# Two decoder layers and two mixers on one core: the first attention as 64 steps in four phases, with the projections cut into pieces inside the steps

## The reference

```python
h = rmsnorm(x, ln1_g[i]) @ w_in[i]
(fq, fk, fv, ff, dq, dk, dv, c_q, c_kv, k_r) = jnp.split(h, split_points, axis=-1)
o_fox = fox_group(fq, fk, fv, ff, fgate_b[i])             # 4 heads of 64, causal, forget bias
o_diff = diff_group(dq, dk, dv, ...)                      # 4 heads, 2 softmaxes each, values of 128
o_mla = mla_group(c_q, c_kv, k_r, ...)                    # 4 heads, 64 + 32 rotary rows, values of 64
x = x + jnp.concatenate([o_fox, o_diff, o_mla], axis=-1) @ w_o[i]
# one block of 128 queries, in every group:
sc = jnp.einsum('bhqd,bhkd->bhqk', qb, k).astype(jnp.float32) * scale
p = jax.nn.softmax(sc + bias_fn(qi, ki), axis=-1).astype(v.dtype)
return jnp.einsum('bhqk,bhkd->bhqd', p, v)
# diff_group, at its end:
o = o1 - lam.astype(o1.dtype) * o2
o = rmsnorm(o, norm_g) * (1.0 - lam_init)
```

## Time and profile before

| | us |
|---|---|
| median of 3 runs (2925.74 to 2937.4) | 2934.0 |
| profiled execution, its own time | 2937.45 |
| its span | 2935.7 |
| PE busy | 2672.3 (91%) |
| DVE, ACT, POOL busy | 1091.8, 985.0, 1032.7 |
| chain that ended last, share of PE | 85% |
| first attention, layer 0, from the first split weight of `cq` to the norm `ln2` | 31.0 to 393.5 |
| the same stages, layer 1 | 775.5 to about 1137 |

### The profile page before, as it was taken

How to read it: one execution, slowest core, us unless ns; L and a number is a source line. 1 busy time by engine, 2 the same in 40 slices (tenths; PEclk the granted TensorE clock), 3 DMA queues, 4 the chain that set the end, 5 groups by cost and what they waited for, 6 DMA issues and landing times.

```text
span 2935.7 us, 34302 instructions
## 1 busy us (share of the span) xinstructions
PE 2672.3 (91%) x13358; PEld 2173.4 (74%) x13358; DVE 1091.8 (37%) x2040; ACT 985.0 (34%) x1811; POOL 1032.7 (35%) x567
## 2 busy tenths in 40 slices
PE   6989889999998988999968999999999899898888
PEld 4866678888776667888846877887878787786666
DVE  2035359730202544984015022241011243255564
ACT  3324344432332434444223132221223222244442
POOL 4341245664434114566442222222322132321121
PEclk9977899999998789999988999999999999999999
DMA  4210135322321013532321100111110021120000
GB/s 157 82 34 1 51 131 193 122 97 90 106 88 41 1 37 120 189 136 90 101 67 44 51 15 22 51 58 58 58 36 29 8 65 57 45 75 29 29 30 29
DMA packets 54513, 199.69 MB, mean 68 GB/s; under 512 B 6288, under 2 KB 6288, under 8 KB 53584
## 3 DMA queue, kind: packets, MB, share of 16 engines
q1 hardware_dynamic: 51696, 188.13, 19.1%
q10 hardware_dynamic: 2656, 9.37, 0.9%
HBM read 194.72 MB, written 2.10 MB: 67 GB/s over the span
## 4 chain that ended last, share of the span: by engine, by line
PE 85%; DVE 5%; ACT 4%; POOL 4%; issue 2%; DMA 0%; ACTq 0%; DVEq 0%; POOLq 0%
PE ps L490 59%; PE ps L520 12%; PE ps L736 5%; PE ps L820 4%; PE ps L619 2%; POOL wl L2033 1%; PE ps L950 1%; ACT wh L987 1%; DVE norm_sq L1520 1%; POOL norm_acc L2046 1%; POOL norm_sq L2149 0%; PE ps L641 0%; PE ps L743 0%; PE ps L935 0%; PE ps L934 0%
## 5 line engine op out<-in xcount | busy, mean ns | idle before, releaser
L2033 POOL TENSOR_TENSOR wl<-wring,wh 128x1024 fp32r<-128x1024 f32 (+2 forms) x305 | 756.8, 2481 | 1302.4 <-ACT wh L987 1291.9
L987 ACT ACTIVATE wh<-wring 128x1024 fp32r<-128x1024 f32 (+2 forms) x305 | 316.6, 1042 | 898.1 <-PE ps L490 889.7
L490 PE MATMUL ps<-hh,wh 128*128 128x512 f32 x1480 | 587.3, 397 | 32.7 <-POOL wl L2033 16.7
L490 PE MATMUL ps<-hl,wh 128*128 128x512 f32 x1480 | 584.9, 395 | 0.0
L490 PE MATMUL ps<-hh,wl 128*128 128x512 f32 x1480 | 584.3, 395 | 0.0
L490 PEld LDWEIGHTS ps<-hh,wh 128*128 128x128 f32 x1480 | 282.3, 191 | 99.0 <-issue 19.2
L490 PEld LDWEIGHTS ps<-hh,wl 128*128 128x128 f32 x1480 | 282.2, 191 | 61.0
L490 PEld LDWEIGHTS ps<-hl,wh 128*128 128x128 f32 x1480 | 282.7, 191 | 58.9 <-issue 0.5
L520 PE MATMUL ps<-arena 128*128 128x512 f32 (+8 forms) x496 | 237.2, 598 | 3.1 <-DVE aq_s L1901 1.5
L1556 DVE CUSTOM_DVE_ANT_0 arena<-arena 128x1024 f32<-128x1024 f32 x96 | 188.7, 1966 | 8.6 <-DVE arena L1690 0.3
L490 PE MATMUL ps<-wh,hh 128*128 128x256 f32 x544 | 156.7, 288 | 12.5 <-POOL wl L2033 4.7
(11 more groups left out here) (266 smaller groups left out, 4538.8 us busy)
## 6 DMA issues: line engine op xcount, KB each, us to landing
wring<-wts SPq DMA_DIRECT2D x284, 512.0 KB, 3.5
arena<-wts SPq DMA_DIRECT2D x48, 512.0 KB, 4.4
wring<-wts SPq DMA_DIRECT2D x18, 384.0 KB, 2.9
xL<-xt SPq DMA_DIRECT2D x1, 2048.0 KB, 9.7
arena<-tab SPq DMA_DIRECT2D x1, 2048.0 KB, 16.7
arena<-cv ACTq DMA_DIRECT2D x2, 1024.0 KB, 4.9
arena<-tab ACTq DMA_DIRECT2D x1, 2048.0 KB, 7.9
out_t<-xL ACTq DMA_DIRECT2D x8, 256.0 KB, 2.0
```

The source lines that it names most:

```text
L490: mm = nc.tensor.matmul(o[0], a, b, start=start and k == first and j == 0, stop=stop and k == last and j == 2)
L987: nc.scalar.activation(wh[:, sn % SPLIT_SLOTS, :kn * w], raw(u)[:, :kn * w], ACT.Copy).then_inc(act_done, tick("act", ("hi", u)))
L2033: G.tensor_tensor(wl[:, sn % SPLIT_SLOTS, :kn * w], raw(u)[:, :kn * w], wh[:, sn % SPLIT_SLOTS, :kn * w].bitcast(F32), ALU.subtract).then_inc(
```

## The change

- **Order of the units.** `unit1` gives four phases of 16 steps: fox, diff heads 0 and 1, diff heads 2 and 3, mla. Inside a phase the query block i is the outer loop, so every phase has its own four steps for each i.
- **Projections in the steps.** Ahead of the steps only cq, ckv, two `qk` jobs, the first `v` job, and the four forget rows remain. A new function `fill1(s)` puts a piece at the end of each PE step: in phases 0 and 1 a quarter of the next phase's `qk` job pair (12 products of 512 columns) or an eighth of its `v` job (12 of 256 columns); in phase 2 `uq`, `ukv`, the turned fox and diff outputs and the first of the output projection; in phase 3 more of it. `wo` is cut by input rows into three parts (features 0 to 511, 512 to 767, 768 to 1023), each added to `xL` by its own DVE add.
- **Differential pairs.** The second softmax of a pair is scaled by -lam times the ratio of the row sums and added to the first, in SBUF (`mix`, three DVE instructions). Only the sum is transposed and multiplied with the values: 48 units of T and PV instead of 64.
- **Fox mask.** The mask comes from PE as one more product (identity by mask, 128 columns) into the scores' bank; POOL's sixteen bias additions are gone.
- **Rotary rows.** The swapped columns are computed by the projection itself (32 more output rows), so the ten transfers and most of POOL's additions are gone; DVE does three 32 x 512 instructions for each mla head instead.
- **Buffers.** The step buffers lie in `arena`, no longer over `wh` and `wl`, so weights are split during the steps. T and PV run one step later (s-3, s-4), and PV has one bank (5) instead of two.

Core of the diff:

```diff
-        add(("ckv", l), "w_in", l, 0, KT, [(CKV, 128), (FG, 4), (None, 60), (KR, 32)])
+        add(("ckv", l), "w_in", l, 0, KT, [(CKV, 128), (FG, 4), (None, 60), (KR, 32), (KR + 16, 16), (KR, 16)])
...
-            add(("wo", l, j), "w_o", l, 0, KT, [(256 * j, 256)])
+            add(("wo", l, 0, j), "w_o", l, 0, 4, [(256 * j, 256)])
+        for part in (1, 2):
+            for j in range(2):
+                add(("wo", l, part, j), "w_o", l, 2 + 2 * part, 2, [(512 * j, 512)])
...
-def units1():
-
-    return ([("fox", h, 0) for h in range(4)] + [("diff", h, c) for h in range(4) for c in range(2)]
-            + [("mla", h, 0) for h in range(4)])
+def unit1(u):
+
+    p, r = divmod(u, 16)
+    i, e = divmod(r, 4)
+    if p in (1, 2):
+        return "diff", i, 2 * (p - 1) + e // 2, e % 2
+    return ("fox" if p == 0 else "mla"), i, e, 0
...
+                def fill1(s):
+
+                    p, r = divmod(s, 16)
+                    if p < 2 and r < 8:
+                        j, (x, i) = 2 + 2 * p + r // 4, divmod(r % 4, 2)
+                        us = views(("qk", l, j))
+                        if x == 0:
+                            claim([6 + i], "act", "qk", l, 2 * j + i)
+                        product(ps[:, 6 + i, :], lat(side(i)), [us[x]], *([("qk", l, 2 * j + i)] if x else []),
+                                *([("used", us[x][0])] if i else []), start=x == 0, stop=x == 1)
...
+                    elif p == 2 and r in (9, 10):
+                        for x in range(2):
+                            turn_out(2 * (r - 9) + x, 6 + x, 0, 1, 2, 3)
+                    elif p == 2:
+                        out_part(0, r - 11, 6 + (r - 11) % 2)
...
-                for s in range(nu + 3 + 6):
+                for s in range(nu + 4):
...
+                        last = nc.tensor.matmul(ps[:, s % 3, 0:ke], a, b, start=True, stop=kind != "fox")
+                        if kind == "fox":
+                            last = nc.tensor.matmul(ps[:, s % 3, ke - 128:ke], idn, arena[:, CM + 384:CM + 512],
+                                                    start=False, stop=True)
...
+                    if s < nu:
+                        fill1(s)
+                    elif s == nu:
+                        turn_out(6, 6, 0, 1, 2)
+                        turn_out(7, 7, 0, 1, 2)
+                turn_out(6, 0, 3)
+                turn_out(7, 1, 3)
+                pe.wait_ge(dve_done, at("dve", "ot", l, 7, 1))
+                for m in range(KT):
+                    out_part(2, m, (2 + m) % 8)
                 norm(("ln2", l))
...
+                splits = {0: (("qk", l, 2), second), 1: (("qk", l, 3), first), 2: (("qk", l, 3), second),
+                          4: (("v", l, 1), first), 6: (("v", l, 1), second), 8: (("qk", l, 4), first),
...
+                          60: (("wo", l, 2, 1),)}
...
+                    u = s - 1
+                    if u in TASK_NO and unit1(u)[0] == "diff":
...
+                        V.reciprocal(q, rs1[:, u % 16:u % 16 + 1]).then_inc(dve_done, tick("dve"))
...
+                        V.scalar_tensor_tensor(out=sbuf[:, u % 4, 0:ke], in0=sbuf[:, u % 4, 0:ke], scalar=q,
+                                               in1=sbuf[:, (u - 1) % 4, 0:ke], op0=ALU.mult, op1=ALU.add).then_inc(
+                            dve_done, tick("dve", ("mix", l, u)))
```

More of the change, by code:

```diff
@@ L1113, in _, with high_out @@
-                nu = len(units) * NT
-                for s in range(nu + 10):
+                split(("qk", l, 2), first)
+                for t in range(NT):
+                    evacuate_v(0, t, t)
+                def high_out(k, b, *blocks):
+                    act.wait_ge(pe_done, at("pe", "ot", l, k, blocks[-1] // 3))
+                    if k == 0:
+                        act.wait_ge(pe_done, at("pe", "v", l, 2, NT - 1))
+                    c = slice(128 * blocks[0], 128 * blocks[-1] + 128)
+                    name = ("oth", l, k, blocks[-1] // 3)
+                    if 2 <= k < 6:
+                        nc.scalar.activation(hH[:, k, c], ps[:, b, c], ACT.Identity, scale=lamc[:, 6:7]).then_inc(
+                            act_done, tick("act", name))
+                    else:
+                        nc.scalar.activation(hH[:, k, c], ps[:, b, c], ACT.Copy).then_inc(act_done, tick("act", name))
@@ L1170, in _ @@
+                high_out(6, 0, 3)
+                high_out(7, 1, 3)
+                split(("up", l, 0), first)
+                act.wait_ge(dve_done, at("dve", "ot", l, KT - 1, 1))
+                act.dma_start(crow.rearrange("p a b -> p (a b)"), cv).then_inc(crow_loaded, 16)
+                for m in range(KT):
+                    if m == 4:
+                        split(("up", l, 0), second)
+                    square(("ln2", l), m, ("xo", l, 2))
                 root(("ln2", l))
@@ L2025, in _, with split @@
             G = nc.gpsimd
-            def split(key):
-                for u in units_of[key]:
+            def split(key, part=slice(None)):
+                for u in units_of[key][part]:
                     n, k0, kn, w, sn = units_w[u]
```

656 lines of the change are left out of this document (356 added, 300 removed).

## The result

The changed kernel takes 2831.79 us (median of 4 runs, 2827.4 to 2835.9), the kernel before 2935.7 beside it: a ratio of 0.9642, with a 95% interval of 0.9619 to 0.9665. The forecast of 2846 had the direction and the place, and was 14 us too high. The profiled execution has a span of 2830.0 us and a mean granted clock of 0.963 (before 2935.7 and 0.940).

A forecast was written before the change was run, and what follows sets the result against it. PE was taken to bound the steps, at a clock held down by idle holes. Terms summed to 266.7 us a layer against 310.5, -88 in all: 2849.5, less 3.4 for the median, 2846; 8-in-10 range 2805 to 2900, own range 2818 to 2882.

The forecast's parts named there:

- T and PV, 46.8: In the steps: transposes and value products of the 48 remaining units take 46.8 us a layer.
- Pairs, -15.6: In the differential steps: 16 of 64 units lose T and PV, saving 15.6 us a layer.
- Fox mask, +4.0: In the fox steps: 16 mask products of 128 columns at 0.25 us each add 4.0 us a layer.
- Seams, 6: Where pieces follow float32 products: 0.11 us each over some 59 pieces, 6 us a layer.
- Projections, seams and clock together, 137.5 + 6 + 8: Per layer: projection products 137.5 us, seams at pieces 6, low-clock stretches after phase 2's waits and in the drain 8.
- Waits in steps, 9, drain, 3, the norm, 5: Per layer: PE waits in phases 2 and 3 and at turned outputs 9 us, drain after the steps 3, norm 5.
- the turned outputs: Eight turned attention outputs per layer, at about 0.44 us each (four transposes), make 3.5 us.
- The worse end of the range: Lower end of the forecast's own gain of 26 to 58 us a layer, 2882 us in time.
- So the steps are bound by PE, at a clock that the holes keep down: Kernel before, attention steps: PE bounds them, and idle holes of 13.1 and 9.4 us hold the clock at 0.77.
- The rival built on it, 2890: Steps: waits keep the clock in part low, mean 0.88, a layer saves 22 us, time 2890; chance 0.12.
- The third rival, lockstep: Steps held 0.5 us each by the ACT and DVE round: 2892 us; chance 0.10, shared with late weights.
- the slower case: Steps: clock stays at 0.77, a layer loses 13 us, time 2960; chance 0.07.

The follow-up runs named there:

- e1: The changed kernel with T and PV of every differential pair issued twice: 2848.24 us, ratio 0.9702 to the kernel before.
- e6: The changed kernel with the fox mask added on GpSimd instead of as a TensorE product: 2820.13 us, ratio 0.9603 to the kernel before.
- e5: The changed kernel with phase 2's latent queries and keys made in turn over its first eight steps: 2828.31 us.
- e4: The changed kernel with the sum of squares for norm ln2 on VectorE instead of GpSimd: 2831.92 us.
- e2: The kernel before, with 42 extra unused 512-column products filling its first hole: 2929.44 us, ratio 0.9975.
- e9: The kernel before, with transposes, products with the values and outputs of every unit one step later: 2900.6 us, ratio 0.9868.
- e10: e8 without the fox mask's product, so the fox heads have no causal mask: 2856.62 us, ratio 0.9718 to the kernel before.
- e8: The changed kernel with the 16 projection pieces of phase 0 issued ahead of the first step: 2830.33 us, ratio 0.9640 to the kernel before.
- e12: The changed kernel with T two steps behind S and PV three, instead of three and four: 2829.76 us.
- e11: e8 with T two steps behind S and PV three, as in the kernel before: 2822.0 us, ratio 0.9603 to the kernel before.
- e3: The changed kernel without the fox mask's product, so the fox heads have no causal mask: 2818.8 us, ratio 0.9605 to the kernel before.

## Why the prediction was right, and what it had wrong

**PE bounds the steps, and a step is the sum of its products.** Right, and it carried the forecast: the lengths of S from rows 5 came back to 0.01 us, T and PV of four blocks too. The terms below are compared with layer 0 after, each group of rows added up from start to start from 83.0 to 340.3 us, PE's waits taken out.

**T and PV, 46.8.** Measured 41.0, the largest miss. For fewer blocks than four the forecast was too high: the chain has 0.11 + 0.17, 0.22 + 0.39 and 0.33 + 0.62 for one to three, together 1.84 where it had 2.47. Its 0.87 for two blocks came from the step at 242.09, whose PV is of a unit with 128 columns of values, while the rows for three and four blocks have units with 64. By starts a PV ahead of a piece is also 0.12 us shorter than one ahead of S (0.82 for 0.94 with four blocks), which the seams below give back.

**Pairs, -15.6.** Too high: e1 gives 8 to 11 a layer. It did not spoil the sum, since the sum was built from what is left, not from what went.

**Fox mask, +4.0.** Right: 0.25 each by e6, for all that a row of the profile after says 0.42. From start to start the sixteen take 5.0, the seam to the first T among it.

**Seams, 6.** Too low. The 0.11 that the forecast read is there, but a piece has two seams, one to the float32 products ahead and one to those behind:

```profile
157.98 0.48 PE L527 MATMUL ps<-hh,wh 128*128 128x512 f32 x1
158.29 0.39 PE L527 MATMUL ps<-hl,wh 128*128 128x512 f32 x1
...
160.60 0.39 PE L527 MATMUL ps<-hh,wl 128*128 128x512 f32 x1
160.92 0.48 PE L704 MATMUL ps<-arena 64*128 64x128 f32 x2
```

Twelve products take 2.94 us (160.92 - 157.98) where they take 2.74 in a row at 0.228 each: 0.20 for the two, and it is the same (2.91 to 2.95) behind S, behind the mask and behind T and PV, in phases 0 and 1 and in e6. Twelve of 256 columns take 1.60 for 1.42. The 2.77, 2.82 and 2.73 of the chains differ because they book the seam ahead to the row before. Only 48 of the 59 pieces are split projections; with six products and 96-row scores the two seams make 0.10. That is some 8 us a layer by my estimate.

**Projections, seams and clock together, 137.5 + 6 + 8.** Measured 146.9, and 1.0 more in S (44.9 for 43.9): 3.6 less than forecast. In the steps there is almost no loss of clock: 1.00, 1.00, 1.00 and 0.96 in the four phases. It lies at the ends: the first `v` job takes 12.9 us against 11.8, and the last 48 products 13.5 against 10.9 at 0.228 each. With some 2.6 for phase 3 and the drain (an estimate from 0.96 and 0.91 over their 45.9 and 8.8 us), the low clock cost 6.3 where the forecast had 8.

**Waits in steps, 9, drain, 3, the norm, 5.** PE is idle 3.5 us in phase 2, 2.9 in phase 3 and 2.3 in the drain, and 5.7 before the norm: 14.3 for 17. The place was right (phase 2's first steps, 2.2 us by e5), and e4 shows that moving the norm's sums gains nothing.

**The sum.** 5.8 + 3.6 + 2.7 too much, against 1.0 for the mask and 1.7 for the turned outputs (5.2 for 3.5) too little: 9.4 us a layer, 266.7 for 257.3. Layer 1 gained 53.7 to its norm, layer 0 53.2. So the two layers gained some 18 us more than forecast, and the 3.4 that the forecast took off for the median did not appear (the profiled execution took 2831.81, the median 2831.79): 18 - 3.4 is its error of 14. Errors on both sides cancelled in part. The worse end of the range is not what the text's own squares give, 44 - 36 = 8 us a layer or 2918 us; it took 26, or 2882.

**The cause of the low clock.** Here the reasoning was wrong, although the number came out. The step that failed is "So the steps are bound by PE, at a clock that the holes keep down": filling the first hole left the clock at 0.50 (e2). Short waits inside the steps have a part: the falls at 265 and 309 us in the kernel before begin behind waits of 1.90 and 1.81, a later order that took them away gave 35 to 37 us (e9), and e10, with two short waits in bare steps, took 26 more than e8. But they are not the whole of it. In e2 waits of 1.89 and 1.81 us left the clock at 1.00, in e8 one layer fell and the other did not behind the same waits, and the changed kernel itself has 0.94, 1.16 and 1.36 in phase 2 at 1.00. Most of the first 48 us of steps stay at half the clock even in e9, where those waits are shorter or gone. What the changed kernel has is no wait at all in phases 0 and 1: with a piece in it a step is 2.6 to 4.7 us long, at either distance (e12), and ScalarE and VectorE are done before T comes due. Its 8 us for the clock were thus near the truth for a reason that does not hold, which is luck. Why it keeps the full clock where the kernel before did not stays open; e8, e11 and e12 show that neither the pieces of phase 0 nor the distance are needed for it.

Of the rule weighed in the prediction (the Trainium skill, "TensorE: Matmul & The Clock Gate", "A second HAM failure mode: psum-queue depth-cycling"), the runs show: with banks changing hands in each of the 64 steps, and seams at 48 split pieces, phases 0 to 2 ran at 1.00. The rival built on it, 2890, the first in the prediction's list, did not come. e10 agrees with the Trainium skill's picture, in that section, of a gate that falls for short idles: waits of 0.29 and 0.38 us stand ahead of 26 us at 0.50. e2 does not, with 1.00 behind 1.89.

The third rival, lockstep, did not come in phases 0 and 1 (PE idle 0), and the slower case needs a mean clock of 0.81 over the steps, where it was 0.99.

## What to carry to other kernels

Build the time of a fused loop from the lengths of what remains in it, start to start at the full clock: that sum held to 4%, with some errors cancelling, while the estimate of what was removed was off by a third to a half. A wait of one or two us on PE may cost several times itself in clock afterwards, or nothing, so look for the short waits inside a dense stretch before blaming the long hole ahead of it; moving the waiting unit a step later is the cheap test. A row of a chain books the seam to whichever instruction stands ahead of it: price a product by leaving it out, or from start to start, not by its row.

## What the runs showed of the hardware

- A low granted clock lasts through work without idle: in e10 from 132 to 172.6 us behind waits of 0.29 and 0.38 (a row of it: 0.50 with PE busy 26.00 of 26), 12 us in the kernel before behind one wait of 1.90, and 24 us in e9 (214 to 238, PE busy 24.00).
- The same wait may bring the low clock or not: 0.50 behind 1.90 and 1.81 us in the kernel before, 1.00 behind 1.89 and 1.81 in e2; 0.50 behind 0.56 in e2, 1.00 behind 0.56 in the kernel before, each in both layers.
- A float32 product of 128 rows and 128 columns costs 0.25 us within a step (e6), and 0.42 by the row of the chain.
- Less work was slower: e10 leaves 32 products out and takes 26 us more than e8, while e3, with pieces between its steps, leaves the same ones out and takes 13 less than the changed kernel.
- Twelve 512-column products of a split projection between float32 products take 2.94 us, 0.20 more than in a row, whatever stands ahead of them (phases 0 and 1, e6).
